# One more unit of the experts' weights beside the ring, and a last pass with the third tile's y entered first

## The chip, the core and the metric

The kernel runs on one core of one Trainium2 chip. The metric is the device time of one execution in microseconds, as a median of runs. The engines are TensorE (PE), VectorE (DVE), ScalarE (ACT), GpSimd (POOL) and SyncE (SP); here SP sends nearly all transfers, into one DMA queue that 16 DMA engines serve.

## What is computed

One step of a hybrid encoder layer on 384 tokens (256 of a new stream, 8 x 16 of running ones), in float32: a mixer (one input projection, a recurrent branch and a spatial gating branch, two projections, an output projection), and then a mixture of 32 experts of which each token takes 4, a residual, and a final RMSNorm. The change touches the experts and the end:

```
x = x + mixer(rms_norm(x))
logits = rms_norm(x) @ w_router + b_router;  gates = softmax(top 4 of 32)
gate_up = hb @ w_gate_up[e] + b_gate_up[e]            # (1024 x 2048) per expert
act = (clip(up) + 1) * (min(gate, 7) * sigmoid(1.702 * gate))
out = act @ w_down[e] + b_down[e]                     # (1024 x 1024) per expert
x = x + sum of gate_e * out_e over the token's experts
y = rms_norm(x) * final_norm_g
```

## The kernel before

**Stages.** First the mixer: its weights come in 28 pieces of 1 MB into two buffers `raw` and are split into high and low parts. Then the router, the choice of experts and their order by size on the chip. Then passes over experts, most with two experts side by side, each for 64 of the 128 rows of a pass. At the end the final norm and the stores.

**Units and the ring.** The weights of one expert are 12 units of 1 MB (8 of gate and up, 4 of down), so a pass of two experts has 24, and its units alternate between the two. The units pass through a ring of 18 slots of 8 KB per partition (`RINGS`). Slot 0 is called `wexp_low`, slot 17 `wexp_high`, the slots between are paired to `wexp0` to `wexp7`, so that two neighbouring units of one expert come in one transfer of 2 MB. Unit 12 has a buffer of its own, `beside` (`BESIDE = 12`): it takes no slot. The place of a unit in the ring's order is therefore its number up to 11, and its number less one from 13 on (`first_place`, L101); the slot is the place modulo 18. Slot 17 shares its memory with `act_l` (an operand of the mixer) and `bdn_hl` (the bias of the down products), `act_t` and the router's `yt` share theirs at offset 176128.

**The order of loads.** SP's program is one list. During the mixer it sends units 0 to 10 when the memory under their slots is free (L365, the helper `load_expert`), then the stores of the state, then waits for these stores and sends `beside` (L408), then units 11 and 13 to 17. From unit 19 on it waits for `wexp_used`, the number of units that TensorE has used. In the first pass TensorE raises this number by 2 after each block of gate and up or down; in later passes by 4 after every second block. `load_pass` (L426) sends the pairs of the passes from the second on: for the pair (u, u + 1) it waits until `wexp_used` is at least u - ring + 2, where `early_ring` gives 19 for units below 30 and 18 from there. In the second pass it stops after four pairs, waits for the first pass's three tiles of the down bias (`combined`, L460), sends unit 18 into slot 17 and goes on.

**A pass on TensorE** (`experts_pass`, L1700): eight blocks k of gate and up (L1751) with the bias behind the first (L1763); behind blocks 1 and 3 the combine of the pass in front (`add_up`, `combine`, L1655 to L1660), in which each token's results of that pass are picked by a matrix product into two PSUM banks; then the gather for the next pass (L1643), the turn of the activations (L1693) and four down blocks (L1819). VectorE adds a combine's two banks to y (L1278) and counts `y_added`. The banks of the three tiles' combines are 4, 6 and 4 (`COMBINE_BANKS`), so the third waits for the first's add.

**The last pass** differs: y itself is entered into the six banks in which the last combine will be summed (`keep_tokens`, L1696, a product with the identity; tile t has banks 2t and 2t + 1), tile 2 behind block 3, tiles 1 and 0 around the turns. The combine of the pass in front stands behind blocks 1 (tiles 0 and 1) and 2 (tile 2). The last combine (L1845) then adds to what stands there, and the final norm reads the banks.

Of the kernel before, what the change touches and what calls it, by code (L numbers as in the profile page):

```python
# [34 lines left out]
P = 128  # L35
D = 1024
# [57 lines left out]
def landings(place):  # L94

    if place % 2 == 1 or place % RINGS == 0:
        return place // RINGS + 1
    return sum(1 for f in FINE for q in range(PLACES[f], min(PLACES[f + 1], place + 1)) if q >= 0 and q % RINGS == place % RINGS)


def first_place(n):  # L101

    return n if n < BESIDE else n - 1

# [19 lines left out]
def hawk_gmlp_moe_streaming_step(  # L124
# [6 lines left out]
    with ExitStack() as ctx:  # L131
# [13 lines left out]
        wexp = [at("wexp_low", RING_AT[0], [P, 2 * D])] + wexp + [at("wexp_high", RING_AT[-1], [P, 2 * D])]  # L145
        beside = at("beside", 106496, [P, 2 * D])
        x_in = at("x_in", 126976, [P, TT, D])
        lru_r = at("lru_r", 65536, [P, CB // 2, T])
# [83 lines left out]
        cnt = at("cnt", 185472, [P, NE])  # L232
        sorted_ = at("sorted", 176128, [P, NE])
        left = at("left", 176256, [P, NE])
        key = at("key", 185600, [P, NE])
# [122 lines left out]
        def _(sp):  # L358
# [32 lines left out]
            sp.dma_start(y[:, 2, :], x_sample.rearrange("b s d -> (b s) d")).then_inc(y_loaded, 16)  # L391
            sp.wait_ge(mrg_ready, CB)
            load_expert(5)
            load_expert(6)
# [15 lines left out]
            load_expert(11)  # L410
            load_expert(13)
            sp.wait_ge(unit_used, MIX_U)
            for n in range(14, RINGS):
                load_expert(n)

            for n in range(RINGS + 1, RINGS + 3):
# [38 lines left out]
            def early_ring(unit):  # L455

                return lambda n: RINGS + 1 if unit + n < RINGS + BESIDE else RINGS

            load_pass(LOADS[1], 0, second, early_ring(LOADS[1]), end=8)
            sp.wait_ge(combined, TT)  # L460
            load_expert(RINGS)
            load_pass(LOADS[1], 0, second, early_ring(LOADS[1]), begin=8)
            for it in range(2, OVER_AT):
# [438 lines left out]
        def _(dve):  # L902
# [370 lines left out]

            def add_to_tokens(it, t):

                dve.wait_ge(combined, it * TT + (t + 1))
                b = COMBINE_BANKS[t]
                dve.tensor_tensor(y[:, t, :], y[:, t, :], ps[:, b:b + 2, :].rearrange("p a b -> p (a b)"), ALU.add).then_inc(y_added, 1)  # L1278

            def experts_pass(it, used, loads, split, table_rows=(), half=False):  # L1280

                for t in range(TT):
                    add_to_tokens(it, t)
                for row in table_rows:
# [44 lines left out]
            for it in range(OVER_AT, NU):  # L1329
                experts_pass(groups_on * OVER_GROUP + it, groups_on * (OVER_GROUP * EXP_U) + LOADS[it], len(UNITS[it][0]),  # L1330
                             split_of(it + 1) if it < LAST else None, half=UNITS[it][1] is HALF)
            dve.wait_ge(y_added, (groups_on * OVER_GROUP + LAST) * TT + TT)

# [43 lines left out]
        def _(pe):  # L1377
# [276 lines left out]

            def combine(it, t):  # L1655

                for k in range(2):
                    o = ps[:, COMBINE_BANKS[t] + k, :]
                    pe.matmul(o, pick_tg[:, t * P:(t + 1) * P], out_h[:, UC * k:UC * k + UC], start=True, stop=False)  # L1659
                    i_ = pe.matmul(o, pick_tg[:, t * P:(t + 1) * P], out_l[:, UC * k:UC * k + UC], start=False, stop=True)  # L1660
                i_.then_inc(combined, 1)
# [7 lines left out]
            def add_up(it, first, tiles):  # L1669

                if first:
                    pe.wait_ge(gat_ready, 1)
                else:
                    pe.wait_ge(out_ready, it)
                    pe.wait_ge(pick_tg_ready, it)
                    pe.wait_ge(y_added, it * TT)
                for t in tiles:
                    if t == 2:
                        pe.wait_ge(y_added, it * TT + 1)
                    if first:  # L1680
                        down_bias(t)
                    else:
                        combine(it - 1, t)

# [15 lines left out]
            def experts_pass(it, unit, later, experts, shape, first, last, fine=False, fine_next=False):  # L1700
# [6 lines left out]

                def weights(k, x):

                    if first and experts * k + x == BESIDE:  # L1710
                        return beside
                    return wexp[place(k, x) % RINGS]

                def landed(k):

                    for x in range(experts):
                        if first and experts * k + x == BESIDE:
                            pe.wait_ge(beside_landed, 16)
                            continue
                        slot, count = place(k, x) % RINGS, 16 * landings(place(k, x))  # L1720
                        pe.wait_ge(exp_landed[slot], later * 16 + count if later is not None and slot in OVER_SLOTS else count)
# [8 lines left out]
                if first:  # L1730
                    pe.wait_ge(xt_first, 1)
                else:
                    pe.wait_ge(tg_ready, it + 1)
                    pe.wait_ge(xt_ready, it * 2 + 2)
                for k in range(CB):
                    if fine or k % 2 == 0:
# [7 lines left out]
                    for b in (0, 2) if half else (0, 2, 1, 3):  # L1744
# [4 lines left out]
                        for n, (s0, w, x) in enumerate(strips(shape)):  # L1749
                            at_ = UC * (b + n) if half else UC * b  # L1750
                            i_ = pe.matmul(ps[s0:s0 + w, b, :], xt[:, k, s0:s0 + w],  # L1751
                                           weights(k, x)[:, at_:at_ + UC], start=k == 0, stop=k == CB - 1)
                            if k == CB - 1 and b == 2 and (n == 0 if half else n == len(strips(shape)) - 1):
# [5 lines left out]
                    if k == (3 if first else 0):  # L1759
# [7 lines left out]
                        if first:  # L1767
# [4 lines left out]
                            i_.then_inc(post_mm, 1)  # L1772
                    if k == (5 if first else 1):
                        add_up(it, first, (0, 1))
                    if k == (6 if first else 2 if last else 3):
                        add_up(it, first, (2,))
                    if last and k == 3:
                        pe.wait_ge(y_added, it * TT + TT)
                        keep_tokens(2, 0)
                        keep_tokens(2, 1)  # L1780

# [3 lines left out]
                if last:  # L1785
                    pe.wait_ge(up_clipped, it * 2 + 1)
                    keep_tokens(1, 0)
                turn(it, 0, 6 if last else 0, fine, 2 if half else 1)
# [15 lines left out]
                for m in range(CB // 2):  # L1804
# [5 lines left out]
                    for kk, c in ((0, 0), (1, 0), (0, 1), (1, 1)) if by_columns else ((0, 0), (0, 1), (1, 0), (1, 1)):  # L1810
# [4 lines left out]
                        for n, (s0, w, x) in enumerate(strips(shape)):  # L1815
                            if half and n != c:
                                continue
                            act_ = act_t[:, k % 4, SLOTS * (k // 4):SLOTS * (k // 4) + SLOTS] if half else act_t[:, k, s0:s0 + w]
                            i_ = pe.matmul(ps[s0:s0 + w, 6 + c, :], act_, weights(CB + m, x)[:, D * kk + UC * c:D * kk + UC * c + UC],  # L1819
                                           start=k == 0, stop=k == CB - 1)  # L1820
# [19 lines left out]
            pe.wait_ge(pick_tg_ready, done)  # L1840
            pe.wait_ge(y_added, done * TT)
            for t, c in LAST_ORDER:
# [32 lines left out]
```

## Time and profile before

| | us |
|---|---|
| median of 3 runs | 1216.59 |
| lowest, highest | 1215.15, 1217.0 |
| the profiled execution | 1215.63 |
| its span, first to last instruction | 1213.5 |

| engine | busy us | share |
|---|---|---|
| PE (matmul) | 1175.4 | 97% |
| DVE | 392.3 | 32% |
| ACT | 232.8 | 19% |
| POOL | 82.7 | 7% |

The DMA queue of SP moved 439.91 MB, 88.1% of what 16 engines could have been busy. A busy share is an average over stages: the first quarter of the span is the mixer, the rest the passes. The chain that ended last is followed back from the last instruction, at each step to what released it. In the table by stretches, the columns are the length, the busy time of each engine, the granted TensorE clock (1.00 is full), the DMA's share of its 16 engines and what it moved in GB/s.

### The profile page before, as it was taken

The numbers are of one execution on the slowest core, as the hardware profiler recorded it, in microseconds if no ns is written. First come the engines' busy times: TensorE is split into PE (matmuls) and PEld (weight loads), VectorE is DVE, ScalarE is ACT, GpSimd is POOL, SyncE is SP. The second block draws the span as 40 slices with busy tenths as digits, with TensorE's granted clock in tenths as the row PEclk, the third lists the DMA queues.
The fourth block names the chain that finished last, engine by engine and source line by source line (L and its number), as shares of the span: only waits on it lengthen the run. The fifth ranks groups of instructions, "written<-read, shape, count | busy, mean of one in ns | idle before, by whom it ended". The sixth has DMA issues, their size and how long they took to land.

```text
span 1213.5 us, 16290 instructions
## 1 busy us (share of the span) xinstructions
PE 1175.4 (97%) x6511; PEld 667.1 (55%) x6511; DVE 392.3 (32%) x667; ACT 232.8 (19%) x399; POOL 82.7 (7%) x243
## 2 busy tenths in 40 slices
PE   9999999999999999899999989999999998999997
PEld 7999999985535354343434343535445343553533
DVE  5648587654252413021211111111212111121213
ACT  5533783233101010000101010101001010110103
POOL 4100000010101001101100010101011010110000
PEclk9999999999999999899999999999999999999999
DMA  7543246589999999999999999999999999999996
GB/s 232 176 154 111 98 139 235 206 318 376 419 422 427 426 427 424 425 427 426 424 428 427 426 424 421 421 420 427 426 429 424 427 426 427 427 425 428 426 424 248
DMA packets 55391, 443.70 MB, mean 366 GB/s; under 512 B 5356, under 2 KB 5452, under 8 KB 24336
## 3 DMA queue, kind: packets, MB, share of 16 engines
q1 hardware_dynamic: 53952, 439.91, 88.1%
q0 software_dynamic: 1216, 2.68, 0.9%
q8 instruction: 51, 0.84, 0.3%
q14 instruction: 28, 0.23, 0.0%
q10 hardware_dynamic: 144, 0.04, 0.0%
HBM read 440.63 MB, written 1.98 MB: 365 GB/s over the span
## 4 chain that ended last, share of the span: by engine, by line
PE 84%; DMA 12%; issue 1%; DVE 1%; ACT 1%; POOLq 0%; POOL 0%; ACTq 0%; DVEq 0%; SPq 0%
PE ps L1751 30%; PE ps L1819 18%; DMA wexp<-in_w_gate_up_dram 12%; PE ps L1643 7%; PE ps L1380 7%; PE ps L1382 7%; PE ps L1381 7%; PE ps L1659 2%; PE ps L1660 1%; PE ps L1693 1%; PE ps L1651 1%; PE ps L1763 1%; PE ps L1605 0%; DMA rows<-in_conv_w_dram 0%; PE ps L1698 0%
## 5 line engine op out<-in xcount | busy, mean ns | idle before, releaser
L1751 PE MATMUL ps<-wexp,xt 128*64 128x512 f32 (+1 forms) x2048 | 462.0, 603 | 16.8 <-DMA wexp<-in_w_gate_up_dram 11.7
L1751 PEld LDWEIGHTS ps<-wexp,xt 128*64 128x64 f32 (+1 forms) x2048 | 144.7, 132 | 261.4 <-issue 260.7
L1819 PE MATMUL ps<-wexp,act_t 128*64 128x512 f32 (+1 forms) x1104 | 227.0, 593 | 4.2 <-issue 4.2
L1819 PEld LDWEIGHTS ps<-wexp,act_t 128*64 128x64 f32 (+1 forms) x1104 | 82.1, 131 | 134.2 <-issue 134.1
L1278 DVE TENSOR_TENSOR y<-y,ps 128x1024 f32<-128x1024 f32 x51 | 60.8, 1219 | 209.4 <-PE ps L1660 200.5
L838 ACT ACTIVATE g<-g 128x512 f32<-128x512 f32 x33 | 20.8, 630 | 546.3 <-DVE g L1292 546.3
L1380 PE MATMUL ps<-act_h,split 128*128 128x384 f32 x352 | 117.8, 335 | 0.0
L1382 PE MATMUL ps<-act_h,split 128*128 128x384 f32 x352 | 117.6, 334 | 0.0
L1381 PE MATMUL ps<-act_l,split 128*128 128x384 f32 x352 | 117.6, 334 | 0.0
L1643 PEld LDWEIGHTS ps<-pick,xn 128*128 128x128 f32 x768 | 91.1, 196 | 14.8 <-issue 14.8
L1643 PE MATMUL ps<-pick,xn 128*128 128x128 f32 x768 | 94.1, 283 | 1.7 <-POOL pick L589 1.7
L1316 DVE SCALAR_TENSOR_TENSOR out_l<-ps,gate_now,out_h 128x1024 fp32r<-128x1024 f32 x16 | 20.5, 1284 | 224.7 <-ACT out_h L854 224.7
L914 DVE TENSOR_TENSOR split<-raw,split 128x2048 fp32r<-128x2048 f32 x29 | 66.3, 2289 | 66.3 <-ACT split L663 66.2
L1292 DVE TENSOR_SCALAR g<-ps 128x512 f32<-128x512 f32 x33 | 22.7, 688 | 174.0 <-PE ps L1751 174.0
L663 ACT ACTIVATE split<-raw 128x2048 fp32r<-128x2048 f32 x29 | 55.6, 1919 | 84.6 <-PE ps L1382 69.3
L1380 PEld LDWEIGHTS ps<-act_h,split 128*128 128x128 f32 x352 | 66.1, 188 | 0.6 <-issue 0.6
L1381 PEld LDWEIGHTS ps<-act_l,split 128*128 128x128 f32 x352 | 66.1, 188 | 0.0
L1382 PEld LDWEIGHTS ps<-act_h,split 128*128 128x128 f32 x352 | 66.1, 188 | 0.0
L1751 PE MATMUL ps<-wexp_high,xt 128*64 128x512 f32 (+1 forms) x152 | 57.9, 606 | 4.5 <-DMA wexp<-in_w_gate_up_dram 4.5
L1751 PE MATMUL ps<-wexp_low,xt 128*64 128x512 f32 (+1 forms) x160 | 59.8, 594 | 0.0
L854 ACT ACTIVATE out_h<-ps,gate_now 128x1024 fp32r<-128x1024 f32 x16 | 17.8, 1114 | 211.4 <-PE ps L1819 211.4
L1659 PE MATMUL ps<-out_h,pick_tg 128*128 128x512 f32 x96 | 41.3, 430 | 0.0
(327 smaller groups left out, 969.8 us busy)
## 6 DMA issues: line engine op xcount, KB each, us to landing
wexp<-in_w_gate_up_dram SPq DMA_DIRECT2D x92, 2048.0 KB, 25.6
wexp<-in_w_down_dram SPq DMA_DIRECT2D x48, 2048.0 KB, 27.3
wexp<-in_w_gate_up_dram SPq DMA_DIRECT2D x38, 1024.0 KB, 25.7
wexp<-in_w_down_dram SPq DMA_DIRECT2D x20, 1024.0 KB, 12.9
raw<-in_w_in_dram SPq DMA_DIRECT2D x19, 1024.0 KB, 5.1
wexp_low<-in_w_gate_up_dram SPq DMA_DIRECT2D x17, 1024.0 KB, 26.3
wexp_high<-in_w_gate_up_dram SPq DMA_DIRECT2D x16, 1024.0 KB, 24.4
wexp_low<-in_w_down_dram SPq DMA_DIRECT2D x5, 1024.0 KB, 22.2
```

Of the source, the lines that this page charges most:

```text
L663: act.activation(split_h[:, n % MIX_SPLIT], raw[:, n % MIX_RING], ACT.Copy).then_inc(high_done, 1)
L838: act.activation(g1[:, j], g1[:, j], ACT.Silu, scale=ALPHA).then_inc(silu_done, 2 if half else 1)
L914: dve.tensor_tensor(split_l[:, n % MIX_SPLIT], raw[:, n % MIX_RING], split_h[:, n % MIX_SPLIT].bitcast(F32), ALU.subtract).then_inc(low_do ...
L1278: dve.tensor_tensor(y[:, t, :], y[:, t, :], ps[:, b:b + 2, :].rearrange("p a b -> p (a b)"), ALU.add).then_inc(y_added, 1)
L1292: dve.tensor_scalar(g1[:, j], ps[:, j, :], LIMIT, None, ALU.min).then_inc(clipped, n)
L1380: pe.matmul(out, a_h, b_h, start=start, stop=False)
L1381: pe.matmul(out, a_h, b_l, start=False, stop=False)
L1382: return pe.matmul(out, a_l, b_h, start=False, stop=stop)
L1643: i_ = pe.matmul(ps[:, 4 + c // 4, c % 4 * P:(c % 4 + 1) * P], rows_, pick[:, t], start=t == 0, stop=t == TT - 1)
L1659: pe.matmul(o, pick_tg[:, t * P:(t + 1) * P], out_h[:, UC * k:UC * k + UC], start=True, stop=False)
L1751: i_ = pe.matmul(ps[s0:s0 + w, b, :], xt[:, k, s0:s0 + w], weights(k, x)[:, at_:at_ + UC], start=k == 0, stop=k == CB - 1)
L1819: i_ = pe.matmul(ps[s0:s0 + w, 6 + c, :], act_, weights(CB + m, x)[:, D * kk + UC * c:D * kk + UC * c + UC], start=k == 0, stop=k == CB - 1)
```

## The change

Two things change.

Unit 13 gets a place of its own as well, in two halves of 0.5 MB: its gate half in `apart_gate` (memory of slot 17's first half), its up half in `apart_up` (memory of `act_t`). The gate half is sent ahead of unit 5, as soon as the mixer's last operand is no longer read; the up half after unit 18, when the router's products are done. Units 14 to 18 now take places 12 to 16, unit 18 is sent with them, place 17 stays empty, and the ring goes on with unit 19 at place 18 as before. `early_ring` gives 17 for units 30 to 35. The wait for `combined` in the second pass's loads is gone. TensorE waits for all three transfers beside the ring before it uses unit 12 or 13. Two small tiles of the sort (`sorted`, `left`) move out of the way.

In the last pass `keep_tokens(2, ...)` stands ahead of the first block instead of behind block 3. The combine of the pass in front is for tile 0 behind block 1 (bank 6), for tile 1 behind block 2 (bank 6, after tile 0's add), and for tile 2 right behind it onto banks 4 and 5, where y already stands; VectorE adds two tiles instead of three in this pass.

```diff
 def landings(place):
...
+    if place % RINGS == RINGS - 1:
+        return place // RINGS
...
-    return n if n < BESIDE else n - 1
+    return n if n < BESIDE else n - 2 if n <= RINGS else n - 1
...
+        apart = [at("apart_gate", 118784, [P, D]), at("apart_up", 176128, [P, D])]
...
             sp.wait_ge(mrg_ready, CB)
+            sp.dma_start(apart[0][:], exp_one((BESIDE + 1) % 2, BESIDE // 2)[:, 0:D]).then_inc(beside_landed, 16)
             load_expert(5)
...
             sp.wait_ge(unit_used, MIX_U - 1)
             load_expert(11)
-            load_expert(13)
+            load_expert(14)
             sp.wait_ge(unit_used, MIX_U)
-            for n in range(14, RINGS):
+            for n in range(15, RINGS + 1):
                 load_expert(n)
+            sp.wait_ge(logits_mm, TT)
+            sp.dma_start(apart[1][:], exp_one((BESIDE + 1) % 2, BESIDE // 2)[:, D:2 * D]).then_inc(beside_landed, 16)
...
             def early_ring(unit):
 
-                return lambda n: RINGS + 1 if unit + n < RINGS + BESIDE else RINGS
-
-            load_pass(LOADS[1], 0, second, early_ring(LOADS[1]), end=8)
-            sp.wait_ge(combined, TT)
-            load_expert(RINGS)
-            load_pass(LOADS[1], 0, second, early_ring(LOADS[1]), begin=8)
+                return lambda n: RINGS + 1 if unit + n < RINGS + BESIDE else RINGS - 1 if unit + n < 2 * RINGS else RINGS
+
+            load_pass(LOADS[1], 0, second, early_ring(LOADS[1]))
             for it in range(2, OVER_AT):
                 load_pass(LOADS[it], 0, ranked(it), early_ring(LOADS[it]))
...
-            def add_to_tokens(it, t):
+            def add_to_tokens(it, t, b):
 
                 dve.wait_ge(combined, it * TT + (t + 1))
-                b = COMBINE_BANKS[t]
                 dve.tensor_tensor(y[:, t, :], y[:, t, :], ps[:, b:b + 2, :].rearrange("p a b -> p (a b)"), ALU.add).then_inc(y_added, 1)
 
             def experts_pass(it, used, loads, split, table_rows=(), half=False):
 
-                for t in range(TT):
-                    add_to_tokens(it, t)
+                for t in range(TT if split else TT - 1):
+                    add_to_tokens(it, t, COMBINE_BANKS[t] if split else 6)
...
-            def combine(it, t):
+            def combine(it, t, b, onto=False):
 
                 for k in range(2):
-                    o = ps[:, COMBINE_BANKS[t] + k, :]
-                    pe.matmul(o, pick_tg[:, t * P:(t + 1) * P], out_h[:, UC * k:UC * k + UC], start=True, stop=False)
-                    i_ = pe.matmul(o, pick_tg[:, t * P:(t + 1) * P], out_l[:, UC * k:UC * k + UC], start=False, stop=True)
+                    o = ps[:, b + k, :]
+                    pe.matmul(o, pick_tg[:, t * P:(t + 1) * P], out_h[:, UC * k:UC * k + UC], start=not onto, stop=False)
+                    i_ = pe.matmul(o, pick_tg[:, t * P:(t + 1) * P], out_l[:, UC * k:UC * k + UC], start=False, stop=not onto)
                 i_.then_inc(combined, 1)
...
-                def weights(k, x):
+                def weights(k, x, at_):
 
                     if first and experts * k + x == BESIDE:
-                        return beside
-                    return wexp[place(k, x) % RINGS]
+                        return beside[:, at_:at_ + UC]
+                    if first and experts * k + x == BESIDE + 1:
+                        return apart[at_ // D][:, at_ % D:at_ % D + UC]
+                    return wexp[place(k, x) % RINGS][:, at_:at_ + UC]
 
                 def landed(k):
 
                     for x in range(experts):
-                        if first and experts * k + x == BESIDE:
-                            pe.wait_ge(beside_landed, 16)
+                        if first and experts * k + x in (BESIDE, BESIDE + 1):
+                            pe.wait_ge(beside_landed, 3 * 16)
...
+                if last:
+                    pe.wait_ge(y_added, it * TT)
+                    keep_tokens(2, 0)
+                    keep_tokens(2, 1)
...
-                    if k == (5 if first else 1):
+                    if last and k == 1:
+                        pe.wait_ge(out_ready, it)
+                        pe.wait_ge(pick_tg_ready, it)
+                        combine(it - 1, 0, 6)
+                    if last and k == 2:
+                        pe.wait_ge(y_added, it * TT + 1)
+                        combine(it - 1, 1, 6)
+                        combine(it - 1, 2, 4, True)
+                    if not last and k == (5 if first else 1):
                         add_up(it, first, (0, 1))
-                    if k == (6 if first else 2 if last else 3):
+                    if not last and k == (6 if first else 3):
                         add_up(it, first, (2,))
-                    if last and k == 3:
-                        pe.wait_ge(y_added, it * TT + TT)
-                        keep_tokens(2, 0)
-                        keep_tokens(2, 1)
 
                 if not last:
                     pe.wait_ge(y_added, it * TT + TT)
                     gather(it + 1, fine_next)
                 if last:
                     pe.wait_ge(up_clipped, it * 2 + 1)
+                    pe.wait_ge(y_added, it * TT + 2)
```

SP's list around the loads of the second pass, before; `wexp5_56` and `wexp6_57` are the slots of units 30, 31 and 32, 33, `wexp_high_60` is slot 17.

```order
L365 DMA wexp5_56<-in_w_gate_up_dram 128x2048 [waits unit_used]
L365 DMA wexp5_56<-in_w_gate_up_dram 128x2048
...
L444 DMA wexp5_56<-in_w_gate_up_dram 128x4096
L365 DMA wexp_high_60<-in_w_down_dram 128x2048 [waits combined]
L444 ISA [waits wexp_used]
L444 DMA wexp6_57<-in_w_gate_up_dram 128x4096
L444 ISA [waits wexp_used]
L444 DMA wexp7_58<-in_w_gate_up_dram 128x4096
L441 ISA [waits wexp_used]
L441 DMA wexp_high_60<-in_w_gate_up_dram 128x2048
```

After, from the last loads in front of the first pass to the same pairs:

```order
L368 DMA wexp6_57<-in_w_down_dram 128x2048
L368 DMA wexp7_58<-in_w_down_dram 128x2048 x2
L420 DMA apart_up_63<-in_w_gate_up_dram 128x1024 [waits logits_mm]
...
L450 DMA wexp5_56<-in_w_gate_up_dram 128x4096
L450 ISA [waits wexp_used]
L450 DMA wexp6_57<-in_w_gate_up_dram 128x4096
L450 ISA [waits wexp_used]
L450 DMA wexp7_58<-in_w_gate_up_dram 128x4096
L447 ISA [waits wexp_used]
L447 DMA wexp_high_60<-in_w_gate_up_dram 128x2048
```

Unit 18 has moved from between the pairs to the group of two `wexp7_58` loads, the up half stands behind it, and the wait for `combined` is gone. The numbers that the ISA rows wait for are those of `early_ring`.

TensorE at the start of the last pass, before (`y,ident` is `keep_tokens`, `out_h,pick_tg` and `out_l,pick_tg` the combine):

```order
L1734 ISA [waits tg_ready]
L1751 MATMUL ps<-wexp_high,xt 64x512 [waits exp_landed1,exp_landed17,xt_ready]
...
L1659 MATMUL ps<-out_h,pick_tg 128x512 [waits y_added]
L1660 MATMUL ps<-out_l,pick_tg 128x512
...
L1751 MATMUL ps<-wexp_53,xt 64x512
L1778 REGISTER_ALU
L1698 MATMUL ps<-y,ident 128x512 [waits y_added]
L1698 MATMUL ps<-y,ident 128x512
L1751 MATMUL ps<-wexp_54,xt 64x512 [waits exp_landed9,exp_landed7]
```

After:

```order
L1738 ISA [waits tg_ready]
L1740 REGISTER_ALU [waits xt_ready]
L1700 MATMUL ps<-y,ident 128x512 [waits y_added]
L1700 MATMUL ps<-y,ident 128x512
L1759 MATMUL ps<-wexp_high,xt 64x512 [waits exp_landed1,exp_landed17]
...
L1759 MATMUL ps<-wexp_53,xt 64x512
L1759 MATMUL ps<-wexp_54,xt 64x512 [waits exp_landed9,exp_landed7]
```

The two products with y stand ahead of the first block, whose wait for its weights (`exp_landed1,exp_landed17`) they no longer stand behind.

## Rows read from the trace of the kernel before

**Rows 1.** The page: the DMA's busy tenths in 40 slices; the chain by engine.

```profile
DMA  7543246589999999999999999999999999999996
...
PE 84%; DMA 12%; issue 1%; DVE 1%; ACT 1%; POOLq 0%; POOL 0%; ACTq 0%; DVEq 0%; SPq 0%
```

**Rows 2.** Stretches: length, PE, PEld, DVE, ACT, POOL busy, clock, DMA share, GB/s.

```profile
267.00:270.00 3.00, 3.00 (x20) 2.20 (x13) 0.42 (x1) 0.72 (x2) 0.00 (x0) 1.00 0.48 134
272.00:276.00 4.00, 4.00 (x29) 2.82 (x27) 0.73 (x4) 2.08 (x5) 0.00 (x0) 1.00 0.22 37
276.00:290.00 14.00, 13.84 (x99) 10.17 (x100) 10.43 (x59) 7.87 (x15) 0.19 (x1) 1.00 1.01 420
290.00:292.00 2.00, 2.00 (x12) 0.66 (x10) 0.26 (x2) 0.00 (x0) 0.00 (x0) 1.00 0.96 270
292.00:330.00 38.00, 37.73 (x205) 18.30 (x203) 10.39 (x20) 4.04 (x11) 6.68 (x22) 1.00 1.01 427
331.00:337.00 6.00, 6.00 (x31) 2.41 (x28) 0.00 (x0) 0.00 (x0) 0.00 (x0) 1.00 0.92 341
337.00:480.00 143.00, 140.79 (x700) 61.41 (x697) 56.70 (x115) 12.67 (x27) 8.07 (x26) 1.00 1.01 427
480.00:1193.00 713.00, 688.23 (x3834) 309.88 (x3835) 131.47 (x208) 68.08 (x157) 43.31 (x142) 0.99 1.01 425
```

**Rows 3.** The chain in order of time: start us, us, what.

```profile
286.10 13.88 PE ps L1751 x64
...
309.94 3.58 PE ps L1751 x16
...
317.76 5.85 PE ps L1643 x48
...
325.39 13.95 PE ps L1819 x64
...
1120.16 29.95 DMA wexp<-in_w_gate_up_dram
...
1168.49 1.91 PE ps L1698 x4
...
1188.86 13.92 PE ps L1819 x64
```

**Rows 4.** Waits of PE over the span: total us, times, longest.

```profile
PE ps L1751 <- DMA wexp<-in_w_gate_up_dram: 16.1, 11, 2.8
```

**Rows 5.** SP's timeline, 244 to 333 us: start us, us, what it sends.

```profile
267.38 0.36 SPq L408 DMA_DIRECT2D beside<-in_w_gate_up_dram  x1
274.05 5.21 SPq L365 DMA_DIRECT2D wexp<-in_w_gate_up_dram  x4
...
317.94 0.33 SPq L444 DMA_DIRECT2D wexp<-in_w_gate_up_dram  x1
329.21 0.33 SPq L444 DMA_DIRECT2D wexp<-in_w_gate_up_dram  x1
332.65 0.33 SPq L441 DMA_DIRECT2D wexp_high<-in_w_gate_up_dram  x1
```

**Rows 6.** Issue to landing: L444's two of 317 to 330 us; L408's.

```profile
DMA to landing us min/median/max: 9.6/12.2/14.8
...
DMA to landing us min/median/max: 4.8/4.8/4.8
```

**Rows 7.** DVE's timeline around the mixer's end.

```profile
266.73 0.69 DVE L1114 TENSOR_TENSOR y<-y,ps 128x512 f32<-128x512 f32 x1 [6.01 <-PE ps L1382]
```

**Rows 8.** PE's timeline at the last pass's first block.

```profile
1150.24 0.61 PE L1751 MATMUL ps<-wexp_high,xt 128*64 128x512 f32 x1 [0.74 <-DMA wexp<-in_w_gate_up_dram]
```

**Rows 9.** The gain row's load: SP's timeline, and its landing.

```profile
1186.53 4.25 SPq L489 DMA_DIRECT2D fnb<-in_final_norm_g_dram  x1
...
fnb<-in_final_norm_g_dram SPq DMA_DIRECT2D x1, 512.0 KB, 14.4
```

**Rows 10.** DVE's timeline in the last pass.

```profile
1159.30 2.35 DVE L1278 TENSOR_TENSOR y<-y,ps 128x1024 f32<-128x1024 f32 x2 [7.26 <-PE ps L1660]
```

More of the change, by code:

```diff
@@ L232, in hawk_gmlp_moe_streaming_step @@
         cnt = at("cnt", 185472, [P, NE])
-        sorted_ = at("sorted", 176128, [P, NE])
-        left = at("left", 176256, [P, NE])
+        sorted_ = at("sorted", 183840, [P, NE])
+        left = at("left", 183968, [P, NE])
         key = at("key", 185600, [P, NE])
@@ L1331, in _ @@
                              split_of(it + 1) if it < LAST else None, half=UNITS[it][1] is HALF)
-            dve.wait_ge(y_added, (groups_on * OVER_GROUP + LAST) * TT + TT)
+            dve.wait_ge(y_added, (groups_on * OVER_GROUP + LAST) * TT + TT - 1)
             def multiply(t, c):
@@ L1682, in add_up @@
                     else:
-                        combine(it - 1, t)
+                        combine(it - 1, t, COMBINE_BANKS[t])
             def turn(it, j, bank, fine, n=1):
@@ L1751, in experts_pass @@
                             i_ = pe.matmul(ps[s0:s0 + w, b, :], xt[:, k, s0:s0 + w],
-                                           weights(k, x)[:, at_:at_ + UC], start=k == 0, stop=k == CB - 1)
+                                           weights(k, x, at_), start=k == 0, stop=k == CB - 1)
                             if k == CB - 1 and b == 2 and (n == 0 if half else n == len(strips(shape)) - 1):
@@ L1818, in experts_pass @@
                             act_ = act_t[:, k % 4, SLOTS * (k // 4):SLOTS * (k // 4) + SLOTS] if half else act_t[:, k, s0:s0 + w]
-                            i_ = pe.matmul(ps[s0:s0 + w, 6 + c, :], act_, weights(CB + m, x)[:, D * kk + UC * c:D * kk + UC * c + UC],
+                            i_ = pe.matmul(ps[s0:s0 + w, 6 + c, :], act_, weights(CB + m, x, D * kk + UC * c),
                                            start=k == 0, stop=k == CB - 1)
@@ L1840, in _ @@
             pe.wait_ge(pick_tg_ready, done)
-            pe.wait_ge(y_added, done * TT)
+            pe.wait_ge(y_added, done * TT - 1)
             for t, c in LAST_ORDER:
```

## Prediction

> **What bounds the kernel now.** I read the page first: the DMA share of the 40 slices and the chain by engine [rows 1]. The chain says TensorE 84%, but from slice 10 to slice 39 the DMA queues are full as well, so the chain alone doesn't say which of the two sets the end. The second view is the table by stretches [rows 2]: from 292 to 330 us the DMA moves 427 GB/s, from 480 to 1193 us 425 GB/s at a share of 1.01. At that rate one unit (1 MB, 1.0486e6 bytes) takes 2.456 us, a pass of 24 units 58.9 us. A whole pass takes TensorE less: passes begin at 286.1 and at 339.3 (325.39 + 13.95), 53 us apart, with a down part of 13.95 us [rows 3]. So TensorE starts with a lead and loses it: it waits for weights 11 times, 16.1 us in all, and the last such wait on the chain is for a transfer that lands at 1150.1 (1120.16 + 29.95) [rows 3, 4]. After 337 us the DMA has no gap until 1193. So what decides is how many bytes were through at 337 us: a byte that is late there is late at 1150.
>
> Between 265 and 337 us the DMA isn't full everywhere [rows 2]. In 272:276 it moves 37 GB/s: SP waits for the last-but-one piece of the mixing weights before it sends unit 11 at 274.05 [rows 5]. In 290:292 it moves 270 GB/s, short by (1 - 270/427) x 2 = 0.74 us. In 331:337 it moves 341 GB/s, short by (1 - 341/427) x 6 = 1.21 us: the ring is full and SP waits for slots. Units 32 and 33 go out at 317.94, 34 and 35 only at 329.21, when the first down block has been used (325.39 + 13.95/4 = 328.9) [rows 3, 5]. The transfer of 317.94 lands 14.8 us later [rows 6], at 332.7: that queue is only just deep enough to bridge the 11.3 us in which no slot comes free.
>
> **The change part by part.** First the gain in front. The gate half of unit 13 (0.5 MB) goes ahead of unit 5; it pushes the stores of the state and the unit beside the ring back by 1.23 us, into the empty stretch before 274.05 (beside is sent at 267.38 and is in 4.8 us later, 272.2 [rows 5, 6]; 1.23 us more still leaves 0.7 us). VectorE, which reads what GpSimd's transfers of the same time bring, has 6.01 us of idle time for it before 266.73 [rows 7]. Gain: 1.23 us. After 274.05 come units 11, 14 to 18 and the up half: 6.5 units where there were 6. That fills the hole at 290: gain 0.74 us. Nothing in front of TensorE waits for it: unit 13 is needed with unit 12 at 309.9 [rows 3], and the up half is in by about 292.
>
> Now the loss. What matters is the count of used units that SP waits for before each pair. Before, the place that unit 30 takes had been freed by 14 used units; after, with units 12 and 13 both outside, places 12 to 16 hold units 14 to 18, and the line asks for unit - 15 instead of unit - 16. In the first pass the count moves by 2 with each block, so pair (30, 31) waits for 16 and not 14, (32, 33) for 18 and not 16, (34, 35) for 20 and not 18; from unit 36 on both kernels ask the same. The 16 is reached at 317.7 and the 18 at 328.9: between them stand the gather, the turn and the first down block. So pair (32, 33) moves from 317.94 to 329.2, and place 17 stays empty until unit 36: at 317.9 the new kernel has 32 units out, the old one 34.
>
> The account of the DMA, step by step. A transfer that meets an empty queue needs time to flow: after the issue at 267.38, 3 us at 134 GB/s hold 0.94 us of full rate, so it flows as from 269.06, 1.68 after the issue; after 274.05, 4 us at 37 GB/s hold 0.35, so from 275.65, 1.6 after it [rows 2, 5]. I take 1.65. Hence:
> - 275.65 + 6.5 x 2.456 + 0.23 (276:290 runs at 420) = 291.8: up half in.
> - Units 19 to 29, 11 x 2.456: until 318.9.
> - Pair (30, 31), out at 317.9, flows from 319.6: a gap of 0.7; until 324.5.
> - Pair (32, 33), out at 329.2, flows from 330.9: a gap of 6.4.
> - From there SP has slots (332.65, where it sent unit 36, now sends three units), so no gap follows.
> New gaps 7.1, old gaps 0.74 + 1.21 = 1.95, less 1.23 for the half unit in front: the DMA is 3.9 us later from 331 us on. Ends of this term: if the old kernel's shortfall at 331:337 comes back, 3.9 + 1.2 = 5.1; if both pairs flow as soon as they are sent, the first gap goes and the second runs from 323.8 to 329.2: 5.4 - 1.95 - 1.23 = 2.2. I take 3.9, since the start-up time is read twice from rows.
>
> By the Trainium skill, DMA: Bandwidth & Descriptors, section Specifications, the first byte of a transfer issued from SP flows after about 0.6 us; an estimate with that figure for both pairs (gap from 323.8 to 329.8) makes the term 2.8 instead of 3.9, and the time 1218.6. The rows speak against it here, because what counts is the full rate on all queues, and that comes 1.6 to 1.7 us after the issue.
>
> Is it given back? TensorE's lead is no help: it is gone at 1150 whatever happens at 331, and the DMA between 337 and 1193 has no idle time in which to catch up. At the start of the second pass (339.3) units 24 to 27 are long in, so TensorE's early passes don't move, and neither do SP's slots.
>
> The last pass. The four instructions of the two products that put tile 2 into its banks take 1.91 us on the chain at 1168.49 [rows 3]. They move ahead of the first block, where TensorE is idle for 0.74 us before 1150.24, waiting for weights [rows 8]. So 0.74 us of them is hidden and 1.17 is paid there: gain 0.74. It is 0 if the final weights are what the end waits for, and 1.9 if the wait ahead of the block is longer. The weights' last column group is used from 1188.86 + 7/8 of 13.92 = 1201.0; the gain row, 0.5 MB and last in the queue, lands at 1200.9 (1186.53 + 14.4), so the weights at about 1199.7 [rows 3, 9]: room for it. All of it keeps its place relative to the DMA, which is later by the same 3.9. The new wait of tile 1's combine for tile 0's add is covered: two adds take 2.35 us together [rows 10] and the third block, in front of that wait, 3.65. Queued behind that wait are the combines of tiles 1 and 2. The add that VectorE loses (about 1.2 us) is hidden behind blocks, so it brings nothing.
>
> Sum: +3.9 - 0.74 = +3.16 us. The profiled execution took 1215.63 us (span 1213.5), so 1218.8; it lay 1.0 below the median of 1216.59, on which the forecast is made: 1219.7.
>
> **The rivals.**
> A, the queue bridges it (faster). One more megabyte stands in front and the queue never runs dry between 318 and 331. For it: landings in 14.8 us show a queue that is deep at 318. It decides where the queue holds more than 331 - 318 = 13 us of work at the issue of pair (30, 31); by my account it holds 1 us of older work and that pair's 4.9. Price: -1.23 - 0.74 (the hole at 290) - 0.74 = -2.7, so 1213.9.
> B, given back (no change). The DMA runs late, but TensorE is what the end waits for, as the chain's 84% says. For it: from 286 to 560 us no wait for weights stands on the chain. Against it: the wait that ends at 1150.1. Half of 3.9 given back and 0.74 gained: +1.2, so 1217.8.
> C, slower still. The uneven end of 331:337 returns and the last pass saves nothing: +5.1, so 1221.7. Against it: SP sends three units at 332.65 while the pair is flowing.
> D, the change doesn't do what it says: the half units take longer than half of a unit, or the moved products push the first block back by their full 1.91, and what the front gains is lost there: -0.74 to +1, if the ring term were not there, 1215.8 to 1217.6. Against it: the counts that SP waits for are numbers in the code.
>
> **How the numbers follow.** Forecast 62%, A 8%, B 12%, C 12%, D 6%. The forecast's own range is 1218.3 to 1221. 0.2% is 2.4 us, about what a measurement of this kernel tells from no change: slower means above 1219.0. Of the forecast four fifths lie above it (0.50), with C 0.12 and a little of the others 0.01: slower 0.63. Faster: A, 0.08. Same: the rest, 0.29. The range that holds 8 in 10: 1216.8 to 1221.9.
>
> **What would show it.** The pair on wexp6 goes out at about 329 instead of 318, and GB/s is near 0 from 325 to 330. The holes at 272:276 and 290:292 are smaller. Waits of TensorE for weights grow from 16.1 by about 3 us. The last pass begins with the moved products, 3 to 4 us later than now, and takes about 1.9 us less from its first block. If GB/s stays at 427 through 331, A is right; if it doesn't and the landing at 1150 isn't later, B.

## The result: slower by 0.3%, as forecast

The changed kernel takes 1219.52 us (median of 12 runs, 1219.02 to 1221.0), the kernel before 1216.01 us (12 runs, 1214.56 to 1217.96). The ratio is 1.0030, 95% interval 1.0022 to 1.0038, so +3.6 us, between +2.7 and +4.6. Forecast were +3.16 us and 1219.7. The sum came out close. Its larger term, the ring, held; of its smaller one, the last pass, at most 0.5 of the 0.74 us are there, and only in executions in which TensorE keeps its full clock, as the runs and profiles below show.

The profiled execution after took 1219.6 us with a span of 1217.6; by it the change cost 4.1 us, half a microsecond more than the medians say: the execution profiled before lies 0.4 us under its median, the one after 0.1 above.

The page after, the rows that answer to [rows 1], and the GB/s of the 40 slices of 30.4 us:

```profile
DMA  7543236589899999999999999999999999999996
GB/s 231 178 152 114 94 139 238 211 325 395 333 429 427 428 424 426 426 426 426 424 428 427 425 425 421 421 422 427 426 428 426 426 427 427 426 426 428 427 422 245
...
PE 81%; DMA 15%; issue 1%; DVE 1%; ACT 1%; POOLq 0%; POOL 0%; ACTq 0%; DVEq 0%; SPq 0%
```

Slice 10 (from 304 to 335 us) falls to 333 GB/s; slices 8 and 9 are a little fuller than before. Behind slice 10 the rates differ by 7 GB/s at most. The stretches of the kernel after, which answer to [rows 2] (columns as there):

```profile
267.00:270.00 3.00, 3.00 (x20) 2.22 (x13) 0.41 (x1) 0.72 (x2) 0.00 (x0) 1.00 0.37 60
272.00:276.00 4.00, 4.00 (x29) 2.84 (x28) 0.75 (x4) 2.08 (x5) 0.00 (x0) 1.00 0.39 123
276.00:290.00 14.00, 13.84 (x99) 10.16 (x100) 10.43 (x58) 7.85 (x15) 0.19 (x1) 1.00 1.01 415
290.00:292.00 2.00, 2.00 (x12) 0.64 (x10) 0.23 (x2) 0.00 (x0) 0.00 (x0) 1.00 1.04 426
318.00:325.00 7.00, 7.00 (x62) 7.00 (x60) 2.54 (x5) 2.69 (x8) 0.00 (x0) 1.00 0.92 372
325.00:331.00 6.00, 5.74 (x29) 2.33 (x31) 1.02 (x6) 0.71 (x3) 3.25 (x10) 1.00 0.24 46
331.00:337.00 6.00, 6.00 (x31) 2.40 (x29) 0.00 (x0) 0.00 (x0) 0.00 (x0) 1.00 0.94 390
337.00:480.00 143.00, 140.80 (x699) 61.51 (x696) 56.57 (x115) 12.67 (x27) 8.10 (x26) 1.00 1.01 427
480.00:1193.00 713.00, 682.55 (x3818) 308.79 (x3818) 130.29 (x207) 68.07 (x157) 43.67 (x142) 0.99 1.01 426
```

The hole at 290:292 is closed (426 GB/s). From 325 to 331 us there are 46 GB/s: of 6 us, (1 - 46/427) x 6 = 5.35 us are lost; 318:325 loses 0.9, 331:337 0.52. That is 6.8 us against 7.1 forecast. From 337 on both kernels move the same. Microsecond by microsecond, the columns as above:

```profile
328.00:329.00 1.00, 1.00 (x8) 0.47 (x6) 0.00 (x0) 0.00 (x0) 0.72 (x4) 1.00 0.00 0
329.00:330.00 1.00, 1.00 (x7) 0.34 (x4) 0.00 (x0) 0.00 (x0) 0.00 (x0) 1.00 0.00 0
330.00:331.00 1.00, 1.00 (x8) 0.39 (x6) 0.00 (x0) 0.00 (x0) 0.00 (x0) 1.00 1.34 246
```

From 328 to 330 us nothing moves: all that was sent before 329.18 has landed.

SP's timeline after, four of its sends, which answer to [rows 5] (start us, us, what it sends):

```profile
268.73 0.36 SPq L412 DMA_DIRECT2D beside<-in_w_gate_up_dram  x1
317.91 0.33 SPq L450 DMA_DIRECT2D wexp<-in_w_gate_up_dram  x1
329.18 0.33 SPq L450 DMA_DIRECT2D wexp<-in_w_gate_up_dram  x1
332.61 0.33 SPq L450 DMA_DIRECT2D wexp<-in_w_gate_up_dram  x1
```

`beside` goes out 1.35 us later than before (forecast 1.23), pair (30, 31) at 317.91 and pair (32, 33) at 329.18.

The last passes after, from TensorE's timeline, which answer to [rows 8] and to the product rows of [rows 3]; in brackets the idle time before and what ended it:

```profile
1125.28 7.09 PE L1759 MATMUL ps<-wexp,xt 128*64 128x512 f32 x32 [2.21 <-DMA wexp<-in_w_gate_up_dram]
1140.00 13.95 PE L1832 MATMUL ps<-wexp,act_t 128*64 128x512 f32 x64 [0.26 <-issue]
1153.88 1.98 PE L1700 MATMUL ps<-y,ident 128*128 128x512 f32 x4
...
1174.32 13.95 PE L1759 MATMUL ps<-wexp,xt 128*64 128x512 f32 x64 [0.26 <-DMA wexp<-in_w_gate_up_dram]
```

Before, the same block 4 on the same view:

```profile
1170.33 13.95 PE L1751 MATMUL ps<-wexp,xt 128*64 128x512 f32 x64
```

The moved products begin where the down part ends, and block 0 starts at 1155.80 without a wait. Before, it started at 1150.24 behind a wait of 0.74 [rows 8]. It would be wrong to read from this that TensorE would not have waited there. The transfer that block 0 waits for is the first of five that SP sends from 1123.24 on; the second line is of this one alone, 31.4 us from issue to landing:

```profile
1123.24 24.34 SPq L450 DMA_DIRECT2D wexp<-in_w_gate_up_dram  x5
DMA to landing us min/median/max: 31.4/31.4/31.4
```

So these weights land at 1154.6, 0.7 us after the down part ends at 1153.88. In the old order block 0 would have begun at about 1154.7 (before, it began 0.13 us after the landing), and block 4 at 1174.8, since before it began 20.09 us after block 0; both are estimates from these rows. Block 4 began at 1174.32, so about 0.5 us came back in this execution. It would have been 0.76, but block 4 now waits 0.26 us for its own weights. The trace of the kernel before held this limit: the weights for its block 4, sent at 1142.80, took 26.9 us and landed at 1169.7, 0.6 us ahead of its start at 1170.33.

The account of this execution closes: the transfer for block 0 lands 4.5 us later than before (1150.1), 0.5 comes back, and block 4 starts 4.0 us later, the span being 4.1 longer. Over the span the waits for weights grew from 16.1 to 21.5 us [rows 4], more than the 3 us forecast:

```profile
PE ps L1759 <- DMA wexp<-in_w_gate_up_dram: 21.5, 13, 2.8
```

### The profile page after: what moved, and what is told of

Read it like the earlier page. It is cut to its first block, busy times and chain, and to the rows that moved or that the text cites. A ratio compares the mean times of both kernels' runs of the same rounds, so it can differ in the third digit from the quotient of the medians.

```text
span 1217.6 us, 16288 instructions
## 1 busy us (share of the span) xinstructions
PE 1173.9 (96%) x6511; PEld 667.9 (55%) x6511; DVE 391.1 (32%) x666; ACT 232.8 (19%) x399; POOL 83.3 (7%) x243
## 3 DMA queue, kind: packets, MB, share of 16 engines
q0 software_dynamic: 1216, 2.68, 1.0%
## 4 chain that ended last, share of the span: by engine, by line
PE 81%; DMA 15%; issue 1%; DVE 1%; ACT 1%; POOLq 0%; POOL 0%; ACTq 0%; DVEq 0%; SPq 0%
PE ps L1759 27%; PE ps L1832 18%; DMA wexp<-in_w_gate_up_dram 14%; PE ps L1645 8%; PE ps L1382 7%; PE ps L1384 7%; PE ps L1383 7%; PE ps L1661 1%; PE ps L1695 1%; PE ps L1662 1%; PE ps L1653 1%; PE ps L1771 1%; PE ps L1607 0%; DMA rows<-in_conv_w_dram 0%; PE ps L1392 0%
## 5 line engine op out<-in xcount | busy, mean ns | idle before, releaser
L1759 PE MATMUL ps<-wexp,xt 128*64 128x512 f32 (+1 forms) x2040 | 456.4, 601 | 23.3 <-DMA wexp<-in_w_gate_up_dram 17.9
L1832 PE MATMUL ps<-wexp,act_t 128*64 128x512 f32 (+1 forms) x1112 | 230.3, 593 | 4.2 <-issue 4.2
```

The lines of the kernel that those rows point to most:

```text
L1759: i_ = pe.matmul(ps[s0:s0 + w, b, :], xt[:, k, s0:s0 + w], weights(k, x, at_), start=k == 0, stop=k == CB - 1)
```

## The experiments

All times are medians. The ratio is that to the kernel before on the same chip, with its 95% interval, and the +x us behind it is what this ratio makes of 1216 us. An interval of 0.001 to either side is 1.2 us.

### The front alone

The changed kernel with the last pass as it was:

```diff
-                if last:
-                    pe.wait_ge(y_added, it * TT)
-                    keep_tokens(2, 0)
-                    keep_tokens(2, 1)
...
+                    if last and k == 3:
+                        pe.wait_ge(y_added, it * TT + TT)
+                        keep_tokens(2, 0)
+                        keep_tokens(2, 1)
```

> The changed kernel with the last pass as it was before: units 12 and 13 beside the ring and the later waits of three pairs remain. Theory (the ring term is all of the loss, the last pass gives 0.7 back): pair (32, 33) goes out at about 329, the DMA moves nearly nothing from 325 to 330 us, time +3.9 us against before. Rival (the last pass gives nothing, since the weights of block 4 are what it waits for): +3.5, the whole difference between the two kernels. Rival (the loss sits in the last pass): about -2.

Measured: 1220.26 us, ratio 1.0029 (1.0019 to 1.0038), +3.5. The loss is in the front. The interval, +2.3 to +4.6, holds the theory's +3.9 and the first rival's +3.5, so the time doesn't say what the last pass is worth. In its profile there is no wait ahead of block 0 of the last pass, and the reason is in the pass in front of it:

```profile
1126.27 8.78 PE L1755 MATMUL ps<-wexp,xt 128*64 128x512 f32 x32 [2.69 <-DMA wexp<-in_w_gate_up_dram]
```

These two blocks took 7.09 us in the kernel after; here they took 8.78, at a granted clock of 0.86 from 1120 to 1130. TensorE comes 1.7 us later to block 0 and finds its weights there.

### The last pass alone

The kernel before with the other half of the change, the lines above the other way round, with the combines' order and banks:

> The kernel before with only the last pass changed. Theory as predicted: block 0 starts 1.17 us later, the blocks from 4 on 0.74 us earlier than before, time -0.7 us. Rival, from the profile after (there TensorE waits 0.26 us for weights ahead of block 4 of the last pass, 3.9 us later than block 4 began before): the transfer for block 4 lands just when the old kernel reaches it, block 4 can't start earlier, a wait for weights stands ahead of it, and the time is the same within 0.3 us.

Measured: 1217.27 us, ratio 1.0002 (0.9993 to 1.0011). The median speaks for no gain, but 0.9994 (-0.74 us) lies in the interval, so the time alone doesn't decide. Its profile, TensorE's timeline:

```profile
1122.86 8.78 PE L1754 MATMUL ps<-wexp,xt 128*64 128x512 f32 x32 [2.46 <-DMA wexp<-in_w_gate_up_dram]
1139.28 13.95 PE L1827 MATMUL ps<-wexp,act_t 128*64 128x512 f32 x64 [0.26 <-issue]
1153.16 1.98 PE L1697 MATMUL ps<-y,ident 128*128 128x512 f32 x4
```

There is no wait ahead of block 0, nor behind it: from 1122.86 to the end the chain is TensorE's own work, and in it the products cost as much in front as they did behind block 3. This execution too has the 8.78 us, at a granted clock of 0.83. Its weights for block 0 landed at 1152.85, 0.3 us before the down part ended; 1.7 us earlier TensorE would have waited for them. So this profile shows that the move gains nothing in such an execution, and doesn't show what it gains in one with the full clock. The rival as I wrote it (a wait for weights appears ahead of block 4) isn't what happened here; that wait is in the profile after.

### The later waits alone

One number of the kernel before; nothing is loaded earlier, and slots stay free that needn't:

```diff
-                return lambda n: RINGS + 1 if unit + n < RINGS + BESIDE else RINGS
+                return lambda n: RINGS + 1 if unit + n < RINGS + BESIDE else RINGS - 1 if unit + n < 2 * RINGS else RINGS
```

> The kernel before with one number changed: SP waits for one used unit more before the pairs (30, 31), (32, 33) and (34, 35), although the slots are free. Nothing is loaded earlier. Theory: pair (32, 33) goes out at 329.2 instead of 317.9; with unit 18 behind pair (30, 31) the DMA runs dry at about 327 and flows again at 330.9; gaps 1.2 + 4.0 + 0.74 against 1.95, so +4.0 us. Rival (the gap is given back, TensorE sets the end): under +1.5.

Measured: 1220.82 us, ratio 1.0031 (1.002 to 1.0042), +3.8. Its stretch where the queue runs dry:

```profile
325.00:331.00 6.00, 5.74 (x30) 2.32 (x31) 1.30 (x6) 1.00 (x4) 3.25 (x10) 1.00 0.65 227
```

In time (+2.4 to +5.1) the three later waits are enough for the whole loss, and a gap of some microseconds at 328 us is paid at the end, 880 us later.

### Slot 17 filled early

The changed kernel leaves slot 17 empty until unit 36. Here unit 36 goes out ahead of pair (32, 33):

```diff
...
-            load_pass(LOADS[1], 0, second, early_ring(LOADS[1]))
+            load_pass(LOADS[1], 0, second, early_ring(LOADS[1]), end=8)
+            sp.wait_ge(combined, TT)
+            sp.wait_ge(wexp_used, BESIDE + 2)
+            sp.dma_start(wexp[RINGS - 1][:], exp_two(second[0], 3)[:, 0:2 * D]).then_inc(exp_landed[RINGS - 1], 16)
+            load_pass(LOADS[1], 0, second, early_ring(LOADS[1]), begin=8, high_in=True)
```

> The changed kernel, but unit 36, the first to use slot 17, is sent behind pair (30, 31) at about 318 instead of at 333: the slot that stood empty is filled. Theory: the gap ends the same but begins one unit (2.46 us) later, so the time is 2.5 us under the changed kernel: +0.7 to +1 against before. Rival (it isn't the bytes through at 331 but something else that costs, like the wait for two more transfers beside the ring or the last pass): same as the changed kernel, +3.5.

Measured: 1217.41 us, ratio 1.0006 (0.9997 to 1.0015), +0.7: 2.9 us under the changed kernel with one unit more in the queue. In its profile SP sends unit 36 at 318.00, and the dry stretch is short by 3.4 us, (1 - 188/427) x 6, where it was 5.35:

```profile
318.00 0.33 SPq L469 DMA_DIRECT2D wexp_high<-in_w_gate_up_dram  x1
325.00:331.00 6.00, 6.00 (x30) 2.41 (x31) 0.54 (x5) 0.22 (x1) 3.02 (x10) 1.00 0.59 188
```

### Pairs sent as single units

A pair waits for the later of its two slots. Here units 30 to 35 go one by one (the second half of a pair counts a semaphore of its own, for which TensorE waits):

```diff
...
+            def one_of_pair(n, rest):
+
+                m, x, slot = n // 4, n // 2 % 2, (LOADS[1] + n - 1) % RINGS
+                if rest:
+                    sp.wait_ge(wexp_used, LOADS[1] + n - RINGS + 3)
+                    sp.dma_start(wexp[slot + 1][:], exp_two(second[x], m)[:, 2 * D:4 * D]).then_inc(pair_rest[n // 2 - 3], 16)
+                    return
+                sp.wait_ge(wexp_used, LOADS[1] + n - (RINGS if n == 6 else RINGS - 2))
+                sp.dma_start(wexp[slot][:], exp_two(second[x], m)[:, 0:2 * D]).then_inc(exp_landed[slot], 16)
...
```

> The same single units, but slot 17 stays empty until 333 as in the changed kernel. Theory: 33 units through at 331, as with slot 17 filled early and pairs kept, so the same time as that kernel, +0.7 to +1.5 against before. Rival (it was slot 17 that mattered, not the count): +3.5.

Measured: 1217.19 us, ratio 1.0005 (0.9996 to 1.0014), +0.6. Slot 17 as such isn't what matters: another unit in another slot does the same.

Both together:

> The changed kernel with slot 17 filled early (unit 36 at about 314) and with the pairs (30, 31), (32, 33), (34, 35) sent as single units, each as soon as its own slot is free: unit 30 at about 309, 31 and 32 at 318, 33 and 34 at 329. Theory (only the units through when the queue flows again at 331 count, 2.46 us each): 34 units instead of 32 of the changed kernel, the gap shrinks from 6.4 to about 2 us, time 4.5 us under the changed kernel, -1 us against before. Rival (1 MB transfers or the order cost something of their own): like the kernel with slot 17 early, +0.7.

Measured: 1214.97 us, ratio 0.9989 (0.998 to 0.9998), -1.3. This version beats both kernels, the one before by a margin just clear of its interval. Its stretches:

```profile
318.00:325.00 7.00, 7.00 (x60) 6.81 (x58) 2.58 (x4) 2.16 (x6) 0.00 (x0) 1.00 0.99 414
325.00:331.00 6.00, 5.74 (x31) 2.66 (x31) 1.46 (x6) 1.25 (x5) 3.26 (x10) 1.00 0.94 366
331.00:337.00 6.00, 6.00 (x30) 2.42 (x28) 0.00 (x0) 0.00 (x0) 0.00 (x0) 1.00 0.95 381
```

The dry stretch is 0.9 us short instead of 5.35.

### The gate half behind unit 18

```diff
-            sp.dma_start(apart[0][:], exp_one((BESIDE + 1) % 2, BESIDE // 2)[:, 0:D]).then_inc(beside_landed, 16)
             load_expert(5)
...
             for n in range(15, RINGS + 1):
                 load_expert(n)
+            sp.dma_start(apart[0][:], exp_one((BESIDE + 1) % 2, BESIDE // 2)[:, 0:D]).then_inc(beside_landed, 16)
```

> The changed kernel with the gate half of unit 13 sent behind unit 18 instead of ahead of unit 5, so the hole at 272:276 isn't used. Theory: the ring caps what is through at 331 at 32 units whatever was gained in front, so the half unit only eats into the gap: same time as the changed kernel, +3.5 against before. Rival (the terms of the prediction's sum add up one by one): 1.2 us more, +4.7.

Measured: 1219.97 us, ratio 1.0028 (1.0017 to 1.004), +3.4, as the changed kernel. The interval, +2.1 to +4.9, just holds the rival's +4.7 too, so the decision is the profile's. Its gap is shorter by what the front no longer brings:

```profile
272.00:276.00 4.00, 4.00 (x28) 2.73 (x27) 0.50 (x4) 2.08 (x6) 0.00 (x0) 1.00 0.25 53
...
325.00:331.00 6.00, 5.74 (x30) 2.57 (x31) 1.29 (x6) 0.98 (x4) 3.25 (x10) 1.00 0.36 109
```

(109 - 46) GB/s over 6 us is 0.38 MB, most of the half unit. And from 327 to 330 us nothing moves in this kernel either (0 GB/s): with or without the half unit in front, all 32 units have landed before the next pair goes out at 329. Once the queue runs dry at a point that slots fix, what came earlier in front only lengthens the gap.

### The products done twice

```diff
+                    for c in range(2):
+                        pe.matmul(ps[:, 4 + c, :], ident[:], y[:, 2, UC * c:UC * c + UC], start=True, stop=True)
                     keep_tokens(2, 0)
                     keep_tokens(2, 1)
```

> The changed kernel with the two products that put tile 2 into its banks done twice ahead of block 0 of the last pass: 1.9 us more of TensorE there. Theory, corrected (ahead of block 0 TensorE waits for no weights, so the moved products are paid in full and the move gains nothing): +1.7 to +1.9 over the changed kernel, +5.3 against before. Rival (the wait ahead of block 0 hides them, as predicted for the first 0.74 us and more): +0 to +1 over the changed kernel.

Measured: 1221.23 us, ratio 1.0041 (1.0028 to 1.0055), +5.0, 1.4 us over the changed kernel. The intervals of the two overlap, so the time only leans to the theory. The profile of one execution says why it is 1.4 and not 1.9:

```profile
1125.68 7.09 PE L1761 MATMUL ps<-wexp,xt 128*64 128x512 f32 x32 [2.88 <-DMA wexp<-in_w_gate_up_dram]
1140.40 13.95 PE L1834 MATMUL ps<-wexp,act_t 128*64 128x512 f32 x64 [0.26 <-issue]
1154.29 1.99 PE L1742 MATMUL ps<-y,ident 128*128 128x512 f32 x4
1156.11 1.88 PE L1700 MATMUL ps<-y,ident 128*128 128x512 f32 x4
1172.53 17.39 PE L1761 MATMUL ps<-wexp,xt 128*64 128x512 f32 x80
```

The clock stayed full, and the weights for block 0 landed at 1155.01, 0.7 us into the first pair of products. So the theory as I wrote it, that TensorE waits for no weights ahead of block 0, doesn't hold here: the first pair covers such a wait, and the second pair is past it. The last row is blocks 3 to 7, so block 4 began at about 1176.0 (1172.53 + 17.39/5). Its weights had landed at 1174.61, so with one pair it could not have begun before 1174.7: an estimate of 1.3 us for the second pair.

### The runs side by side

Units through when the queue flows again at about 331 us, counted from SP's list, and the time against before:

| kernel | units | us against before |
|---|---|---|
| the change | 32 | +3.6 |
| the front alone | 32 | +3.5 |
| the later waits alone | 32 | +3.8 |
| the gate half late | 32 | +3.4 |
| slot 17 early | 33 | +0.7 |
| single units | 33 | +0.6 |
| both | 34 | -1.3 |
| before | 34, but short at 331:337 | 0 |

From 32 to 34 units the time falls by 3.6 + 1.3 = 4.9 us, 2.45 us a unit. At 427 GB/s a unit takes 2.456. The order of the rows is what is shown; the agreement to a hundredth is luck, for each time has an interval of about 1 us to either side, and the two steps by themselves are 2.9 to 3.0 (32 to 33) and 1.9 to 2.0 (33 to 34).

## Why the prediction was right, and where it wasn't

- **The bound.** Right. A shift at 331 us arrives at the end; the lead that TensorE has in the first passes gives nothing back, and the chain's share of 81 to 84% for TensorE didn't make it the bound.
- **The ring term, +3.9.** Right in mechanism and nearly in size: pair (32, 33) at 329.18 (forecast 329.2), later waits alone +3.8, front alone +3.5. The gaps were 6.8 us for 7.1. In the one execution profiled, the transfers of the last pass landed 4.5 us later than before.
- **The front gain, 1.23 + 0.74.** The holes were filled as worked out, but as terms of a sum they were misleading: without the 1.23 the time is the same within the noise, and the empty queue at 327 to 330 says why. The count of units at 331 gives nearly the same as the 3.9, and more directly: 2 units, 4.9 us, less the 1.21 that the kernel before lost at 331:337, 3.7.
- **The start-up of 1.65 us.** Held nearly: the four microseconds from 330 on hold 246, 213, 393 and 442 GB/s in the kernel after, together 3.0 us of full rate, so it flows as from 331.0, 1.8 us after the issue at 329.18. By the Trainium skill, DMA: Bandwidth & Descriptors, section Specifications, the first byte comes after some 0.6 us. The trace shows 0 GB/s in 329:330, so here no byte moved in the first 0.8 us. The sum by the page's figure gave 2.8 for the term where the runs show 3.5 to 3.8, though their intervals reach down to 2.3; for the return to full rate the row of the trace was the better measure.
- **The last pass, -0.74.** Too large, and right only for some executions. The mechanism worked in the profile after: 0.85 us of the products lie in a wait for weights, as worked out for 0.74. Two things were left out. First, the weights for block 4 cap the gain: they landed 0.6 us before the old block 4 began, and in the profiles after and of the single units block 4 now waits 0.26 and 0.25 us for them. That leaves 0.5. Second, in these profiles TensorE is idle ahead of block 0 only where its clock stayed full behind the wait in the pass in front. I had one execution to read it from [rows 8]. Of ten profiles four are like it; in the other six the two blocks behind that wait took 8.78 us for 7.09, the weights for block 0 landed 0.3 to 1.0 us before TensorE came to it, and the move gives nothing. How many executions are of either kind isn't known, so the term is between 0 and 0.5. With 0 to 0.5 in place of 0.74 the sum is +3.4 to +3.9, and +3.6 was measured.
- **The rivals.** A fails on the empty stretch, B on the table above. C's +5.1 lies outside the interval, which ends at +4.6, though its part on the last pass (it saves nothing) holds for the executions with the lower clock. D's times, up to 1217.6, are below every run of the changed kernel.

Open: what the last pass is worth in the median, for the interval of its own run is 1.1 us to either side. Open too why the last transfers were 4.5 us later in the profile and not 3.9, and why the clock falls behind one wait and not behind another like it.

## What to carry to other kernels

In a kernel whose queue is full for hundreds of microseconds, count what is through at the last moment at which the queue can run dry; everything else in front of that moment is worth nothing, and each unit there is worth its transfer time at the end. A buffer beside a ring is only a gain if the ring's own slots are as full as before: moving a tenant out shifts all places behind it, and with transfers that need two slots the later one sets the time. A wait of less than a microsecond that one profile shows may not be there in the next execution: look at several before you hide work in it. And look when the weights of the blocks behind it land, for they cap what can be gained.

## What the runs showed of the hardware

The same wait can bring a lower clock in one execution and none in another. Behind 2.46 us of idle time in the run of the last pass alone, the 32 matmuls of two blocks took 8.78 us instead of 7.09, and the granted clock of that stretch was 0.83, so for part of it at the lower of the two levels (1.2 of 2.4 GHz). The same stretch of the changed kernel, behind 2.21 us, kept the full clock:

```profile
1120.00:1130.00 10.00, 7.54 (x28) 2.79 (x28) 0.04 (x1) 0.00 (x0) 0.00 (x0) 0.83 1.01 431
```

```profile
1120.00:1130.00 10.00, 7.79 (x38) 2.70 (x36) 0.00 (x0) 0.00 (x0) 0.00 (x0) 1.00 1.00 424
```

The first row is of the last pass alone, the second of the changed kernel. The idle time alone doesn't sort them. The clock stayed full behind 0.84 (before), 1.94 (single units), 2.21 (the change) and 2.88 us (the products twice). It fell behind 2.19 (slot 17 early), 2.46 (the last pass alone), 2.69 (the front alone), 2.70 (the later waits alone), 2.81 (both) and 2.88 us (the gate half late), and each of these six took 8.78 us for the two blocks.

The 1.7 us stand on the chain, but not all of them are paid. In the four profiles with the full clock the weights for block 0 of the last pass land 0.6 to 0.7 us after the down part ends; in the six others they land before it. So the slower blocks eat the wait that would come at block 0.
